# Block and layer ends of a two-block network, done by blocks of 128 rows

## The reference

```python
x = layer_norm(ALPHA * x + merged @ w_out, ln_g[0], ln_b[0])      # first block, after its four mixers
y = moe(x, ...)                                                   # 32 experts, 2 per token, each weighed by a gate
x = layer_norm(ALPHA * x + y, ln_g[1], ln_b[1])                   # end of the first block
for l in range(2):                                                # second block, two layers
    h = rms_norm(x, norm_pre[l])
    merged = ...                                                  # five branches; all projections read h
    x = x + rms_norm(merged @ w_out[l], norm_post[l])
```

## Time and profile before

| | |
|---|---|
| median of three runs | 2715.63 us |
| profiled execution: time | 2716.89 us |
| profiled execution: span, first to last instruction | 2714.6 us |
| TensorE matmuls busy | 2273.5 us (84%) |
| VectorE busy | 1421.0 us (52%) |
| ScalarE busy | 852.6 us (31%) |
| mean granted TensorE clock | 0.894 of 2.4 GHz |

### The profile page before, as it was taken

How to read it: one execution, slowest core, us unless ns; L and a number is a source line. 1 busy time by engine, 2 the same in 40 slices (tenths; PEclk the granted TensorE clock), 3 DMA queues, 4 the chain that set the end, 5 groups by cost and what they waited for, 6 DMA issues and landing times. The chain is left out here.

```text
span 2714.6 us, 30529 instructions
## 1 busy us (share of the span) xinstructions
PE 2273.5 (84%) x11222; PEld 1699.1 (63%) x11222; DVE 1421.0 (52%) x2416; ACT 852.6 (31%) x1389; POOL 127.6 (5%) x161
## 2 busy tenths in 40 slices
PE   6546698889984599998099989999858999999986
PEld 4445576556764566765077667877647766787765
DVE  2652345956434466664534467763333446777343
ACT  2110133223221366654233342322223334232221
POOL 0000000300000122321000000000000000000000
PEclk8555699999986699999599999999878999999998
DMA  4100332231113499996432311323114322132311
GB/s 126 75 16 1 112 99 70 63 93 59 62 62 96 99 337 339 338 339 209 157 116 93 75 59 48 105 84 118 66 63 127 106 59 66 41 100 93 128 36 70
DMA packets 283202, 298.97 MB, mean 110 GB/s; under 512 B 61005, under 2 KB 255645, under 8 KB 283017
## 3 DMA queue, kind: packets, MB, share of 16 engines
q1 hardware_dynamic: 273578, 288.53, 33.1%
q0 software_dynamic: 9472, 8.43, 0.9%
HBM read 293.85 MB, written 33.19 MB: 120 GB/s over the span
## 5 line engine op out<-in xcount | busy, mean ns | idle before, releaser
L1488 PE MATMUL acc<-x_hi,w_hi 128*128 128x512 f32 x1632 | 680.0, 417 | 33.1 <-DVE w_lo L1442 28.6
L1489 PE MATMUL acc<-x_lo,w_hi 128*128 128x512 f32 x1632 | 644.5, 395 | 0.0
L1490 PE MATMUL acc<-x_hi,w_lo 128*128 128x512 f32 x1632 | 644.4, 395 | 0.0
L1418 ACT CAST w_hi<-raw 128x1024 fp32r<-128x1024 f32 x212 | 220.8, 1044 | 761.2 <-PE acc L1490 709.1
L1442 DVE TENSOR_TENSOR w_lo<-raw,w_hi 128x1024 fp32r<-128x1024 f32 x203 | 248.0, 1224 | 387.9 <-ACT w_hi L1418 382.3
L1488 PEld LDWEIGHTS acc<-x_hi,w_hi 128*128 128x128 f32 x1632 | 312.6, 192 | 119.1 <-DVE w_lo L1442 29.6
L1489 PEld LDWEIGHTS acc<-x_lo,w_hi 128*128 128x128 f32 x1632 | 312.3, 191 | 75.6 <-issue 14.2
L1490 PEld LDWEIGHTS acc<-x_hi,w_lo 128*128 128x128 f32 x1632 | 311.2, 191 | 68.5
L1498 PE MATMUL br<-y_t,raw_b 128*128 128x512 f32 x448 | 217.3, 608 | 20.1 <-DVE sg L1451 20.1
L1231 DVE TENSOR_TENSOR w_lo<-wgu,w_hi 128x1024 fp32r<-128x1024 f32 x128 | 151.1, 1221 | 118.1 <-ACT w_hi L1187 117.5
L1187 ACT CAST w_hi<-wgu 128x1024 fp32r<-128x1024 f32 x128 | 128.5, 1050 | 118.2 <-DMA wgu<-in_moe_w_up 113.6
(11 more groups left out here) (489 smaller groups left out, 2940.7 us busy)
## 6 DMA issues: line engine op xcount, KB each, us to landing
raw<-in_w_in SPq DMA_DIRECT2D x61, 1024.0 KB, 5.4
raw<-in_w_gate SPq DMA_DIRECT2D x40, 1024.0 KB, 5.4
wgu<-in_moe_w_gate SPq DMA_DIRECT2D x32, 1024.0 KB, 10.2
wgu<-in_moe_w_up SPq DMA_DIRECT2D x32, 1024.0 KB, 13.4
wd<-in_moe_w_down SPq DMA_DIRECT2D x32, 1024.0 KB
...
y_t<-in_w_out SPq DMA_DIRECT2D x6, 2048.0 KB, 8.1
room<-in_x SPq DMA_DIRECT2D x2, 2048.0 KB, 8.8
```

The lines of the kernel that those rows point to most:

```text
L1418: self.nc.scalar.copy(self.w_hi[:, n % 2], self.weights(n)).then_inc(self.rounded, 1)
L1488: pe.matmul(acc, hi, tile.hi[:, k, :], start=(k == 0), stop=False)
L1489: pe.matmul(acc, hi, tile.lo[:, k, :], start=False, stop=False)
L1490: mm = pe.matmul(acc, lo, tile.hi[:, k, :], start=False, stop=(k == KT - 1))
```

## The change

All ends become single stages that go by blocks of 128 rows.

- `OutputRows` is the projection by w_out. The first half of w_out is loaded during the last `merge_stage`, into the room of x. `pe_first` goes by chunk of channels over all four blocks of rows, so that TensorE can begin when one chunk of `merged` and one of w_out is split; `pe_second` goes by block of rows. ScalarE and VectorE split in the order ORDER, four chunks of the first half through a ring in the stream's `w_hi` and `w_lo`.
- `block_end` ends the first block: ALPHA * x + projection, layer norm, store to DRAM (the router's and the experts' x) and turning, each per block of rows while TensorE projects the next. Mean and variance come from ScalarE (Copy and Square with accumulated sums). x is reloaded from the input.
- `pairs_end` replaces `combine_pairs`, `add_rows`, `norm_rows` and the first layer's `norm_rows` and `rows_to_split`. The other branch of the experts' If, not taken with these inputs, writes its result in the form of pairs (`results_to_pairs`).
- `layer_end` ends a layer of the second block: projection, norm_post, residual and store, and after the first layer also norm_pre and the turning into `x_hi` and `x_lo`, and the split of the next layer's first tile (`after`).
- The loop over the two layers is written out. One stream serves both (`restart`, `firsts`), with its first loads in `pairs_end`, and the second layer's in the first one's last merge stage. The last `layer_end` stores straight to the output, 512 KB at a time.
- The loads of the router's weights move to the last merge stage of the first block, those for the memory keys (`MemoryKeys`, 5 MB) from the norm's stage to the router's, and the store of x from `dispatch_table` to `block_end`.

The core of the diff (indentation cut; the waits and the order are as in the kernel):

```diff
-sp.dma_start(x_dram.rearrange("(i p) d -> p i d", p=P), x_rows[:]).then_inc(back, 16)
...
+def pairs_end(c, y_dram, pair, room, rows_to, gain, bias, pre, x_hi, x_lo, opening):
...
 for i in range(NT):
-    for r in range(2):
-        sp.dma_start(rows[:, r, i, :], y_dram[r * S + i * P:r * S + (i + 1) * P, :]
-                     ).then_inc(row_in[i], 16)
+    for n in range(2):
+        sp.dma_start(r[:, n, i, :], y_dram[n * S + i * P:n * S + (i + 1) * P, :]).then_inc(pair_in[i], 16)
+    if i == 0:
+        for j, one in enumerate((gain, bias, pre)):
+            sp.dma_start(gb[:, j, :], one.partition_broadcast(P)).then_inc(gains_in, 16)
+for dst, src, loaded in opening:
+    sp.dma_start(dst, src).then_inc(loaded, 16)
+for i in range(NT):
+    sp.wait_ge(rowed, i + 1)
+    sp.dma_start(rows_to[i * P:(i + 1) * P, :], room[:, i, :]).then_inc(rows_out, 16)
...
+def weigh(i):
+    act.wait_ge(pair_in[i], 32)
+    nc.scalar.activation(r[:, 0, i, :], r[:, 0, i, :], ACT.Copy, scale=pair[:, i, 0:1]).then_inc(weighed, 1)
+act.wait_ge(eps_ready, 2)
+weigh(0)
+weigh(1)
+for s in range(NT + 2):
+    if s < NT:
+        act.wait_ge(summed, s + 1)
+        z = r[:, 0, s, :]
+        run(nc.scalar.activation(sq[:], z, ACT.Copy, scale=-1.0 / D, accum_out=st[:, s, 0:1]))
+        run(nc.scalar.activation(sq[:], z, ACT.Square, bias=st[:, s, 0:1], accum_out=st[:, s, 1:2]))
+        nc.scalar.activation(st[:, s, 2:3], st[:, s, 1:2], ACT.Sqrt, bias=eps[:, 0:1], scale=1.0 / D
+                             ).then_inc(rooted, 1)
+    if s + 2 < NT:
+        weigh(s + 2)
+    if 0 <= s - 1 < NT:
+        act.wait_ge(rowed, s)
+        run(nc.scalar.activation(sq[:], room[:, s - 1, :], ACT.Square, accum_out=st[:, s - 1, 4:5]))
+        nc.scalar.activation(st[:, s - 1, 5:6], st[:, s - 1, 4:5], ACT.Sqrt, bias=eps[:, 1:2], scale=1.0 / D
+                             ).then_inc(pre_rooted, 1)
+    if 0 <= s - 2 < NT:
+        act.wait_ge(turned, s - 1)
+        for half in range(2):
+            nc.scalar.copy(x_hi[:, 4 * half:4 * half + 4, (s - 2) * P:(s - 1) * P], turned_rows(s - 2, half)
+                           ).then_inc(x_rounded, 1)
...
+for s in range(NT + 2):
+    if s < NT:
+        z = r[:, 0, s, :]
+        dve.wait_ge(weighed, s + 1)
+        run(nc.vector.scalar_tensor_tensor(z, r[:, 1, s, :], pair[:, s, 1:2], z, ALU.mult, ALU.add))
+        nc.vector.scalar_tensor_tensor(z, room[:, s, :], ALPHA, z, ALU.mult, ALU.add).then_inc(summed, 1)
+    if 0 <= s - 1 < NT:
+        i = s - 1
+        if i == 0:
+            dve.wait_ge(gains_in, 48)
+        x = room[:, i, :]
+        dve.wait_ge(rooted, s)
+        run(nc.vector.reciprocal(st[:, i, 3:4], st[:, i, 2:3]))
+        run(nc.vector.tensor_scalar(x, r[:, 0, i, :], st[:, i, 0:1], st[:, i, 3:4], ALU.add, ALU.mult))
+        run(nc.vector.tensor_tensor(x, x, gb[:, 0, :], ALU.mult))
+        nc.vector.tensor_tensor(x, x, gb[:, 1, :], ALU.add).then_inc(rowed, 1)
+    if 0 <= s - 2 < NT:
+        i = s - 2
+        for half in range(2):
+            k = slice(4 * half, 4 * half + 4)
+            dve.wait_ge(x_rounded, 2 * i + half + 1)
+            nc.vector.tensor_tensor(x_lo[:, k, i * P:(i + 1) * P], turned_rows(i, half),
+                                    x_hi[:, k, i * P:(i + 1) * P].bitcast(F32), ALU.subtract).then_inc(x_split, 1)
+    if 0 <= s - 1 < NT:
+        i = s - 1
+        dve.wait_ge(pre_rooted, s)
+        run(nc.vector.reciprocal(st[:, i, 6:7], st[:, i, 5:6]))
+        if i >= 2:
+            dve.wait_ge(turned, i - 1)
+        nc.vector.scalar_tensor_tensor(h[:, i % 2, :], room[:, i, :], st[:, i, 6:7], gb[:, 2, :], ALU.mult,
+                                       ALU.mult).then_inc(h_ready, 1)
...
-self.round(act, n + 1)
-if n:
+if n + 1 not in self.firsts:
+    self.round(act, n + 1)
+if n not in self.firsts:
     self.evict(act, n - 1)
...
+raw = x_rows[:].rearrange("p i d -> p (i d)").rearrange("p (n s) -> p n s", s=S)
...
+c.load_beside([(raw, a["w_out"][0][:, 0:512].rearrange("(k p) n -> p k n", p=P)), (wr[:, :, 0:4], a["router_g"][0].rearrange("(k p) e -> p k e", p=P)),
...
+banks.close()
+block_end(c, stream, merged[:], x_hi, x_lo, a["w_out"][0], (raw, y_t[:, 0:8]), x_rows, a["x"][0], merged, dram["x"],
+          a["ln_g"][0, 0], a["ln_b"][0, 0])
...
+class OutputRows:
...
+RING = 4
+ORDER = [0, 1, 2, 3, 4, 8, 9, 5, 10, 11, 6, 12, 13, 7, 14, 15]
...
+def sp(self, sp, w):
+    sp.dma_start(self.raw[1], w[:, 512:1024].rearrange("(k p) n -> p k n", p=P)).then_inc(self.w_in, 16)
+def first_used(self, sp):
+    sp.wait_ge(self.w_split, self.at[KT - 1])
+def pe_first(self, pe):
+    for k in range(KT):
+        pe.wait_ge(self.m_split, k + 1)
+        pe.wait_ge(self.w_split, self.at[k])
+        w_hi, w_lo, _ = self.parts(k)
+        for i in range(NT):
+            acc, rows = self.ps[:, i, :], slice(i * P, (i + 1) * P)
+            pe.matmul(acc, self.hi[:, k, rows], w_hi, start=(k == 0), stop=False)
+            pe.matmul(acc, self.hi[:, k, rows], w_lo, start=False, stop=False)
+            mm = pe.matmul(acc, self.lo[:, k, rows], w_hi, start=False, stop=(k == KT - 1))
+        mm.then_inc(self.used, 1)
+def pe_second(self, pe, i):
+    acc, rows = self.ps[:, 4 + i, :], slice(i * P, (i + 1) * P)
+    for k in range(KT):
+        if i == 0:
+            pe.wait_ge(self.w_split, self.at[KT + k])
+        pe.matmul(acc, self.hi[:, k, rows], self.w_hi[:, k], start=(k == 0), stop=False)
+        pe.matmul(acc, self.hi[:, k, rows], self.w_lo[:, k], start=False, stop=False)
+        mm = pe.matmul(acc, self.lo[:, k, rows], self.w_hi[:, k], start=False, stop=(k == KT - 1))
+    mm.then_inc(self.acc, 1)
...
+def weights(n):
+    hi, _, raw = self.parts(n)
+    if n == KT:
+        act.wait_ge(self.w_in, 16)
+    if self.RING <= n < KT:
+        act.wait_ge(self.used, n - self.RING + 1)
+    nc.scalar.copy(hi, raw).then_inc(self.w_rounded, 1)
+for k in range(KT):
+    merged(k)
+    if k < self.RING:
+        weights(self.ORDER[k])
+for n in self.ORDER[self.RING:]:
+    weights(n)
...
+def layer_end(c, stream, after, merged, x_hi, x_lo, w_out, raw, room, rows_from, rows_to, post, pre):
...
+o.sp(sp, w_out)
+o.first_used(sp)
+for i in range(NT):
+    sp.dma_start(room[:, i, :], rows_from[i * P:(i + 1) * P, :]).then_inc(rows_in[i], 16)
+for i in range(NT):
+    sp.wait_ge(rowed, i + 1)
+    sp.dma_start(rows_to[i * P:(i + 1) * P, :], room[:, i, :]).then_inc(rows_out, 16)
+sp.wait_ge(rows_out, 16 * NT)
...
+o.act(act)
+if after is not None:
+    act.wait_ge(o.used, KT)
+    stream.round(act, after)
+act.wait_ge(o.used, KT)
+for s in range(steps):
+    if pre is not None and 0 <= s - 1 < NT:
+        act.wait_ge(rowed, s)
+        run(nc.scalar.activation(sq[:], room[:, s - 1, :], ACT.Square, scale=D ** -0.5,
+                                 accum_out=st[:, s - 1, 4:5]))
+        act.sem_inc(pre_squared, 1)
+    if pre is not None and 0 <= s - 2 < NT:
+        act.wait_ge(turned, s - 1)
+        for half in range(2):
+            k = slice(4 * half, 4 * half + 4)
+            nc.scalar.copy(x_hi[:, k, (s - 2) * P:(s - 1) * P], turned_rows(s - 2, half)).then_inc(x_rounded, 1)
+    if s < NT:
+        for half in range(2):
+            if half:
+                act.wait_ge(o.acc, s + 1)
+            run(nc.scalar.activation(sq[:, half * 512:half * 512 + 512], o.ps[:, s + 4 * half, :], ACT.Square,
+                                     scale=D ** -0.5, accum_out=st[:, s, half:half + 1]))
+        act.sem_inc(squared, 1)
+        act.wait_ge(var, s + 1)
+        nc.scalar.activation(st[:, s, 3:4], st[:, s, 2:3], ACT.Sqrt).then_inc(rooted, 1)
+    if pre is not None and 0 <= s - 1 < NT:
+        act.wait_ge(pre_var, s)
+        nc.scalar.activation(st[:, s - 1, 6:7], st[:, s - 1, 5:6], ACT.Sqrt).then_inc(pre_rooted, 1)
...
+o.dve(dve)
+if after is not None:
+    stream.rest(dve, nc.vector, after)
+dve.wait_ge(gains_in, 16 * len(gains))
+for s in range(steps):
+    if pre is not None and 0 <= s - 1 < NT:
+        dve.wait_ge(pre_squared, s)
+        nc.vector.tensor_scalar(st[:, s - 1, 5:6], st[:, s - 1, 4:5], 1e-6, None, ALU.add).then_inc(pre_var, 1)
+    if pre is not None and 0 <= s - 2 < NT:
+        for half in range(2):
+            k = slice(4 * half, 4 * half + 4)
+            dve.wait_ge(x_rounded, 2 * (s - 2) + half + 1)
+            nc.vector.tensor_tensor(x_lo[:, k, (s - 2) * P:(s - 1) * P], turned_rows(s - 2, half),
+                                    x_hi[:, k, (s - 2) * P:(s - 1) * P].bitcast(F32), ALU.subtract
+                                    ).then_inc(x_split, 1)
+    if s < NT:
+        dve.wait_ge(squared, s + 1)
+        nc.vector.tensor_scalar(st[:, s, 2:3], st[:, s, 0:1], st[:, s, 1:2], 1e-6, ALU.add, ALU.add
+                                ).then_inc(var, 1)
+    if pre is not None and 0 <= s - 1 < NT:
+        dve.wait_ge(pre_rooted, s)
+        run(nc.vector.reciprocal(st[:, s - 1, 7:8], st[:, s - 1, 6:7]))
+        if s - 1 >= 2:
```

(39 more changed lines are left out.)

484 lines of the change are left out of this document (271 added, 213 removed).

## The result

The changed kernel takes 2631.52 us (median of 4 runs, 2630.74 to 2633.56), the kernel before 2715.70 beside it: ratio 0.9693, 95% interval 0.9676 to 0.9709. The profiled execution took 2630.74, with a span of 2628.9 and 1.8 around it; TensorE's mean granted clock rose from 0.894 to 0.909. Forecast were 2624, own range 2614 to 2634.

A forecast was written before the change was run, and what follows sets the result against it. No engine is full in the four stretches between projections, a relay of stages each waiting for the whole before, so gain comes from overlap. 27.4 + 8.3 + 30.8 + 26.1 = 92.6 us off 2716.89 gives 2624.3; forecast 2624, own range 2614 to 2634.

The forecast's parts named there:

- First block's end: From 772.56 to the router's first matmul: 88.3 us now, exits beside the projection and an earlier start save 27.4.
- the 2.65 I kept: Projection's start: 2.65 us lost by its first matmuls at low clock after the pause, kept though the pause shrinks to 3.8.
- Moved loads at nothing: Last merge stage and router's stage: 2 MB of w_out and 5 MB for memory keys cost nothing; uncovered, 5 and 13 us.
- After the experts: From 1291.62 to the first projection at 1363.88: 72.3 us now, 8.3 saved, with the stage beginning about 1.4 later.
- Between the layers: From 1946.80 to 2049.56: 102.8 us now, 30.8 saved; TensorE waits for the exits' chain.
- The ring between ScalarE and VectorE: Between the layers: exits hand over between both engines in series, 7.7, then 8.8, 8.8 us a block, longer than TensorE's 5.4.
- The end: From 2631.93 to the execution's last instruction: 83.4 us now, 26.1 saved, with the last store 512 KB.
- Stages not touched: Outside the four stretches: the change touches only these; the prediction is wrong if other stages change.
- Longer exits: Rival, 20%: hand-overs in four stages cost 0.4 us more each, with 5 us of moved loads uncovered; 20 back, 2645.
- More gain: Rival, 13%: the clock stays up over the three 3.8 us pauses (8) and the table's store comes 5 earlier; 2610.
- TensorE never at its full clock: Slower rival, 2%: in the three projections TensorE, fed in pieces, takes 0.43 for 0.227 us a matmul; 2732.
- Table loads: Rival, 3%: in `block_end` and `pairs_end` two table loads of 1.28 return for each of 8 blocks, 20.5 us; 2644.

The follow-up runs named there:

- late weights: Changed kernel, but the first half of w_out is loaded at the stage's start and not during the last merge stage: 2653.66 us, ratio to the kernel before 0.9778.
- waiting exits: Changed kernel, but sum, norm and turning wait until all four blocks are projected, in three stretches: 2675.39 us, ratio to the kernel before 0.9858.
- run with turns: Changed kernel with unread turns of the identity on TensorE ahead of each projection and around the first block's end's last two turnings: 2622.32 us, ratio to before 0.9662.
- single store: Changed kernel, but each layer's rows leave in one 2 MB store and not in four of 512 KB: 2635.55 us, ratio to the kernel before 0.9711.

## Why the prediction was right, and where it was not

**First block's end**, 27.4 forecast, 27.6 measured. TensorE began 2.1 after ScalarE, as said; the clock stayed low from 772.7 to 779.5, the 2.65 I kept; no pause in the projection; the load of the second half took till 783.8 and chunk 5 was split about 786, as said. Norm on VectorE 3.45 a block for 3.55. Only one table load in the stage: that rival was wrong. The late weights price the early load (7.3) and the waiting exits the overlap (14.2); no run took the other 6.1 apart, and that they are one norm on shorter ways is my reading.

**Moved loads at nothing.** Right for the merge stage. In the router's stage the loads of the memory keys moved 0.99 of the DMA's time and the matmuls took 13.84 for 12.19, 1.7 longer, but not for them: beside the same loads they took 9.6 in the run with turns. It was the clock, 0.50 for 0.58. Dispatch gave back 0.7, of the 0 to 5 that the store ahead of the table might have cost.

**After the experts**, 8.3 forecast, 4.1 measured: this step failed. I had the stage begin 1.4 later for the meeting behind the branch, from a row (the 1.70 before 1308.26) in which only VectorE was waited for and the rest had long been there; in the changed kernel the branch ends right behind the experts and nothing covers it. The first pair was used 23.0 after the experts' last matmul where I had 17.3: 5.7 late. From there the stage took 55.0 for my 56.6, steps of 10.6 for 11.

What the late start is stands in the kept traces, in the semaphore, drain and branch instructions that the views leave out. From the experts' last matmul to the end of their stage both kernels take 9.8, of which GpSimd's drain behind the last scatter is 5.3. There the kernel before issues its first transfer, at 9.9. The changed kernel first has the empty stage inside the branch, 1.7, nearly all of it 21 semaphore clears on GpSimd (1.5). Then TensorE takes 3.4 over the jump out of the branch, where every other engine takes under 0.1, and the empty stage behind it makes all wait for TensorE: the first transfer is issued at 15.5, 5.6 later and not 1.4. The kernel before has the same jump with 3.6 on TensorE, at 1307.8, but beside VectorE's `add_rows`, which did not have to wait for it: the cost was there and hidden. The two small loads took 1.8 for my 0.8 and the first pair 5.7 from its issue for 5.2. Without the second empty stage SyncE begins 3.4 earlier, as the experiment shows. Transfers of instructions are seen at 1268.7, within the jump (1267.8 to 1271.2); that TensorE waits for them is likely and not shown.

**Between the layers**, 30.8 forecast, 31.8 measured. The ring between ScalarE and VectorE was right to 0.1 in each of three steps (7.7, 8.8, 8.8), and the hand-overs, which I had left at 0, added nothing to that sum; scale from PSUM took 1.54 for 1.3 and the next stage's first matmul came 0.5 after the last split and not 1.2.

**The end**, 26.1 forecast, 23.8 measured. Up to the last add 53.7 for my 52.7: 192 matmuls took 47.3 for 46.4, mostly since those of the second half were 0.233 apart and not 0.227. Why they were is open; in the first block's end they kept 0.227, in every run. From the add's end to the span's 5.1 for 3.9: the last 512 KB moved from 2624.5 to 2626.1, and closing the stage and the program took 2.8 from there where I had 1.1 and the kernel before took 0.8 (its change of stage, 1.4, stood ahead of the store). 1.9 of the 2.8 are 26 semaphore clears on GpSimd in the empty stage that closes the program; in the kernel before none stood behind the store, and shared over four engines they took off 1.0. The single store had the size of the bytes right (4.0 for 3.9).

**Stages not touched**: I said I would be wrong if they changed. The experts' stage took 347.6 us for 345.8, and 347.6 to 349.2 in every other run of mine, so it is no scatter. Its DMA share is 0.98 to 1.01 in both, and it moved 0.7% less per us. Why was not found; no run took it apart.

**The other signs.** Rows of x left the first block 5.5, 6.3 and 3.4 apart for my 5; the next layer's first projection came 71.0 after `layer_end` began for 72; the last matmul ended 9.5 before the span did for 8. The first pairs, measured from the experts' last matmul on the scale of the kernel before, were used at 1304.7, behind the 1302 at which I said I would be wrong. Two slips of my own: the end's 83.4 us are 82.7 (2714.6 less 2631.93; the 26.1 is taken from the right instants), and 2.5 MB at 2.6 us put the second pair 6.5 behind the first and not 6.1 (measured 6.4). The total came out 7.5 slower than 2624, near the upper bound of the range: the good sums of two stretches stand beside misses of 4.2, 2.3 and 1.8.

**The rivals.** Longer exits fell: the steps came out within 0.1. More gain was there to be had, but not in this kernel: the clock can stay up over such a pause, and without work in it fell in all three. TensorE never at its full clock fell (1.00 from 781.5 on). Table loads fell with the one load in the first block's end and one in `pairs_end`.
